# Gate biases of a hybrid block: one 128-row product of rounded parts and remainders in place of a narrow f32 product

## The chip, the cores and the metric

One Trainium2 chip, one core of it. The metric is the device time of one execution in microseconds (us), as the median of several executions. The kernel is one program that runs two transformer blocks, one after the other, on 256 tokens of width 1024.

## The reference

The first block is a three-branch mixer (a short convolution, a sparse attention called NSA, a gated delta net called GDN) and a mixture of experts; the second is a block with latent attention, a dense feed-forward, a state space mixer and a second mixture of experts. What the change touches is the merge of the three branches:

```python
branches = einsum('bsrc,rcd->bsrd', stack([y_a, y_n, y_g], axis=2), w_branch)
gates = sigmoid(h @ w_gate + b_gate).reshape(b, s, 3, dm)      # b_gate: 3072 values
merged = sum(gates * branches, axis=2)
return merged @ w_out
```

Here h is the normed input (256 x 1024), w_gate is 1024 x 3072, and b_gate is added to every token's row before the sigmoid.

## The kernel before, in words

Weights are f32 and come through a ring of four 2 MB slots, loaded by the SP queue (L139) in an order written out by hand. A slot is reloaded once its last reader has signalled. Large products are made in three products of rounded operands (type fp32r): ScalarE rounds a part of the weights to w_hi (L192), VectorE makes the remainder w_lo (L202), and TensorE multiplies hi by hi, lo by hi and hi by lo (L263 to L265).

A gate unit is 512 columns of w_gate for branch r (0 to 2) and half (0 or 1): six gate units, each with four weight parts. `merge_part` (L1132 on) numbers the steps: steps 0 to 3 of a half are the gate parts and steps 4 and 5 the branch parts. `merge_step_pe` does one step: for both token tiles of 128 rows, two chunks of 128 input features, three products each, twelve matmuls of 512 columns in all. In the fourth gate step (n == 3) it also adds the bias: for each token tile one product whose left side is one column of the identity over 6 rows, repeated 128 times, and whose right side is `rows512`, the bias as 6 rows of 512 values. Both are plain f32 (L1156). So there are 12 such products, and the profile shows each as two matmuls. The left side picks row 2r + half and copies it to all 128 tokens.

These steps are not made in one place. They are put between the small products of the serial stages, so that TensorE has work while other engines answer:

- GDN (about 117 to 258 us): branch 0. A triangular matrix is inverted in levels lv = 1 to 6. In each level TensorE makes a product Z, a merge step, two more products (XZ, ZX), and a second merge step, while VectorE subtracts them (`gdn_newton`, L1519 and L1521) and makes the next level's mask (L1486). TensorE waits for L1521 before the next level. The bias falls in the second step of levels 2 and 5.
- NSA (about 258 to 446 us): branch 2, half 0 before the attention, then branch 2, half 1 and the gates of branch 1 beside the 12 attention jobs, one step per job. In a job TensorE makes scores, the merge step, the transposes of the job two before, and the output of the job three before; VectorE scores and finishes (L1789, L1795 to L1804), ScalarE takes exponentials (L1570) and copies (L1583), and both also round weights.
- ScalarE takes the sigmoid of a finished gate (L1188), VectorE multiplies it with the branch into `merged` (L1207 to L1212), whose first write is at about 200 us.

The bias rows come with the 18 small loads that SP issues in `start_sync` behind the first four weight loads; all of them raise the signal `small`, which TensorE and ScalarE await at the start of GDN (L1283, L1387). VectorE's list for GDN (`gdn_dve`, L1436) begins with a wait for ScalarE's `ea`.

After NSA come the last branch products, the output projection, and the first mixture of experts (to about 1000 us). SP issues the first expert loads after every engine has finished NSA.

Of the kernel before, what the change touches and what calls it, by code (L numbers as in the profile page):

```python
# [342 lines left out]
def block(nc, A, out):  # L343
# [5 lines left out]
    def sb(name, shape, dt=F32, where=None):  # L349
        return (where or ctx).enter_context(nc.sbuf_tensor(name, shape, dt))  # L350
# [79 lines left out]
    thin = sb("thin", [P, NT, 32], where=mix)  # L430
    gates = sb("gates", [P, NT, 24], where=mix)
    h_mix = [sb(f"h_mix_{n}", [P, KD, T], F32R, where=mix) for n in ("hi", "lo")]
    rows512 = sb("rows512", [6, 512], where=mix)
    gd = ExitStack()
    qkvT = sb("qkvT", [P, 12, T], where=gd)
    zT = sb("zT", [P, 4, T], where=gd)
# [511 lines left out]
    def start_sync(s):  # L948
# [1 line left out]
            s.dma_start(dst, src).then_inc(*small.up(by=16))  # L950

        s.dma_start(pos_i[:, :], A["positions_2"][0].rearrange("(t p) -> t p", p=P)).then_inc(*positions.up(by=16))
        load(rows512[:, :], A["b_gate"].rearrange("l (r n) -> (l r) n", n=512))
        load(w_thin[:, :, 0:24], rows(w_in[:, O_NG:O_NG + 24]))
        load(w_thin[:, :, 24:32], rows(w_in[:, O_GB:O_GB + 8]))
        load(w_thin[:, :, 32:64], rows(ssm_in[:, 5120:5152]))
# [180 lines left out]
    def merge_step_pe(p, r, step):  # L1137
        half, n, u, part = merge_part(r, step)
        if n == 0 or n == 4:
            if n == 0:  # L1140
                sums_let_go(r, half)
            banks.take(p, "unit", u)
            banks.hold("unit", u)
        ps = banks.held_by("unit", u)
        hi, lo = split.take(p, part)
        h, k0, kt = (h_mix, 2 * n, KD) if n < 4 else (ys_, 2 * n - 8, 4)
        if n == 4:
            p.wait_ge(*branch_made(r))
        for t in range(NT):
            o = ps[:, t * 512:(t + 1) * 512]  # L1150
            for k in range(2):
                ins = split_product(p, o, tiles(h, k0 + k, slice(t * P, (t + 1) * P)), (hi[:, k, :], lo[:, k, :]),
                                    k0 + k == 0, k0 + k == kt - 1 and n > 3)
            if n == 3:
                row = 2 * r + half
                ins = p.matmul(o, ident[0:6, row:row + 1].to_broadcast([6, P]), rows512[:, :], start=False, stop=True)  # L1156
        ins.then_inc(*split.used.up())
        if r != 1 and n == 5:
            banks.let_go("unit", unit["gate", r, half])
        if r == 1 and step in (7, 4):  # L1160
            banks.let_go("unit", unit["gate", 1, 0 if step == 7 else 1])
# [274 lines left out]
    def gdn_dve(v):  # L1436
        st = S["gdn"]
        d = st.dve
        v.wait_ge(*st.act.of("ea"))
        for t in range(NT):  # L1440
            settle(v, v.tensor_tensor(g_[:, t, :], thin[:, t, 28:32], gdn_ab[:, 4:8], ADD), d)
# [2195 lines left out]
```

## Time and profile before

| | |
|---|---|
| median of 3 runs | 2491.43 us (2487.21 to 2493.35) |
| profiled execution, its own time | 2489.03 us |
| its span, first to last instruction | 2487.2 us |
| TensorE matmul busy | 2173.5 us, 12847 instructions |
| VectorE busy | 1424.4 us |
| ScalarE busy | 1157.9 us |
| mean granted TensorE clock | 0.948 |

The span is what the trace covers; the own time is the same execution by the device's timer. Engines are PE (TensorE matmul), PEld (TensorE weight load), DVE (VectorE), ACT (ScalarE), POOL (GpSimd), SPq (the queue of SyncE, which issues DMAs). Matmuls overlap in the array, so the time one takes of the engine is the distance from its start to the next one's start, not the duration in its row. A granted clock of 1.00 is 2.4 GHz, and 0.50 is 1.2 GHz; the clock takes one of the two at any moment, and a value between is the mean of a stretch.

### The profile page before, as it was taken

Reading aid. Unit: us, or ns where it says so; the run is one execution under the profiler, and the core shown is the slowest. Engines: PE = TensorE matmul, PEld = TensorE weight load, DVE = VectorE, ACT = ScalarE, POOL = GpSimd, SP = SyncE. Lnnn points to the kernel's source line nnn. Section 1 sums busy time; section 2 is a strip of 40 time slices with the busy share of each in tenths; the row PEclk is TensorE's granted clock in tenths of the full one; section 3 lists DMA queues with packets and bytes.
Section 4 is the critical chain, followed back from the end, with each engine's and each line's share of the span. In section 5 each row is a group of like instructions: output and inputs, shape, how many; then the busy total and the mean of one; then the engine's idle time right before and its main releaser. Section 6 shows DMA issues by size and latency. Waiting matters only on the chain.

```text
span 2487.2 us, 30921 instructions
## 1 busy us (share of the span) xinstructions
PE 2173.5 (87%) x12847; PEld 1670.1 (67%) x12847; DVE 1424.4 (57%) x1977; ACT 1157.9 (47%) x1520; POOL 43.5 (2%) x107
## 2 busy tenths in 40 slices
PE   7989899886665665889999998989999999999997
PEld 7977767741111112667998887778787787787875
DVE  3844635421111101435455756669888888888897
ACT  4432254210000001443443566547777777787775
POOL 0000200000000000000000000000000000000000
PEclk9999988988888888999999998999999999999999
DMA  8442741679999999376454321339989989989994
GB/s 270 169 172 100 247 176 68 238 314 409 409 409 409 409 409 349 140 289 219 170 187 169 136 102 68 119 127 338 355 329 330 372 315 348 354 317 366 335 335 186
DMA packets 267695, 656.78 MB, mean 264 GB/s; under 512 B 13454, under 2 KB 38546, under 8 KB 267544
## 3 DMA queue, kind: packets, MB, share of 16 engines
q1 hardware_dynamic: 266592, 652.90, 70.8%
q8 instruction: 106, 1.74, 0.3%
q10 hardware_dynamic: 952, 1.77, 0.2%
q14 instruction: 45, 0.37, 0.0%
HBM read 653.60 MB, written 1.05 MB: 263 GB/s over the span
## 4 chain that ended last, share of the span: by engine, by line
PE 68%; DMA 16%; DVE 9%; ACT 5%; issue 2%; POOL 0%; ACTq 0%; DVEq 0%; POOLq 0%; SPq 0%
PE psum L263 17%; PE psum L264 17%; PE psum L265 17%; PE psum L252 8%; DMA ring<-in_w_expert_down 5%; DMA ring<-in_w_expert_up 5%; DMA ring<-in_w_expert_gate 5%; PE psum L2385 2%; DVE w_lo L202 2%; PE psum L1099 1%; PE psum L259 1%; ACT w_hi L192 1%; PE psum L2407 1%; DMA ring<-in_ada_w 1%; PE psum L893 1%
## 5 line engine op out<-in xcount | busy, mean ns | idle before, releaser
L202 DVE TENSOR_TENSOR w_lo<-ring,w_hi 128x1024 fp32r<-128x1024 f32 (+1 forms) x778 | 905.5, 1179 | 383.3 <-ACT w_hi L192 367.8
L192 ACT CAST w_hi<-ring 128x1024 fp32r<-128x1024 f32 (+1 forms) x778 | 785.1, 1015 | 435.5 <-PE psum L265 431.1
L263 PE MATMUL psum<-w_hi,xg_hi 128*128 128x512 f32 (+1 forms) x768 | 294.6, 384 | 1.3 <-ACT xg_lo L2068 1.3
L265 PE MATMUL psum<-w_lo,xg_hi 128*128 128x512 f32 (+1 forms) x768 | 289.4, 377 | 0.0
L264 PE MATMUL psum<-w_hi,xg_lo 128*128 128x512 f32 (+1 forms) x768 | 289.4, 377 | 0.0
L2385 PE MATMUL psum<-ring,hT 128*32 128x512 f32 x960 | 145.9, 738 | 116.7 <-DMA ring<-in_w_expert_gate 64.0
L2385 PEld LDWEIGHTS psum<-ring,hT 128*32 128x32 f32 x960 | 29.6, 122 | 228.4 <-DMA ring<-in_w_expert_up 77.3
L263 PEld LDWEIGHTS psum<-w_hi,xg_hi 128*128 128x128 f32 x768 | 144.7, 188 | 31.1 <-issue 1.7
L264 PEld LDWEIGHTS psum<-w_hi,xg_lo 128*128 128x128 f32 x768 | 144.8, 189 | 29.4 <-issue 1.7
L265 PEld LDWEIGHTS psum<-w_lo,xg_hi 128*128 128x128 f32 x768 | 144.6, 188 | 29.2
L263 PE MATMUL psum<-w_hi,midT_hi 128*128 128x512 f32 x352 | 140.8, 400 | 4.0 <-DVE w_lo L202 4.0
L2237 DVE TENSOR_TENSOR x<-x,psum 128x1024 f32<-128x1024 f32 x14 | 17.1, 1221 | 217.6 <-PE psum L252 217.6
L264 PE MATMUL psum<-w_hi,midT_lo 128*128 128x512 f32 x352 | 139.5, 396 | 0.0
L265 PE MATMUL psum<-w_lo,midT_hi 128*128 128x512 f32 x352 | 139.5, 396 | 0.0
L2407 PE MATMUL psum<-ring,midT 128*32 128x512 f32 x480 | 70.9, 722 | 43.9 <-DMA ring<-in_w_expert_down 43.4
L259 PE MATMUL psum<-ident 128*128 128x128 f32 x624 | 87.6, 304 | 16.3 <-issue 8.7
L263 PE MATMUL psum<-h_f_hi,w_hi 128*128 128x256 f32 x352 | 99.9, 284 | 1.6 <-DVE h_f_lo L811 1.6
L264 PE MATMUL psum<-h_f_hi,w_lo 128*128 128x256 f32 x352 | 99.7, 283 | 0.0
L265 PE MATMUL psum<-h_f_lo,w_hi 128*128 128x256 f32 x352 | 99.6, 283 | 0.0
L259 PEld LDWEIGHTS psum<-ident 128*128 128x128 f32 x624 | 84.2, 218 | 19.3 <-issue 10.6
L263 PEld LDWEIGHTS psum<-w_hi,midT_hi 128*128 128x128 f32 x352 | 66.3, 188 | 20.8 <-issue 5.4
L2420 ACT COPY midT<-psum 128x512 f32<-128x512 f32 x8 | 4.7, 586 | 160.3 <-PE psum L893 160.3
(665 smaller groups left out, 3773.8 us busy)
## 6 DMA issues: line engine op xcount, KB each, us to landing
ring<-in_moe_w_gate SPq DMA_DIRECT2D x40, 2048.0 KB, 9.2
ring<-in_moe_w_up SPq DMA_DIRECT2D x40, 2048.0 KB, 10.0
ring<-in_moe_w_down SPq DMA_DIRECT2D x40, 2048.0 KB, 9.1
ring<-in_w_expert_gate SPq DMA_DIRECT2D x30, 2048.0 KB, 17.3
ring<-in_w_expert_up SPq DMA_DIRECT2D x30, 2048.0 KB, 17.1
ring<-in_w_expert_down SPq DMA_DIRECT2D x30, 2048.0 KB, 18.2
ring<-in_ada_w SPq DMA_DIRECT2D x24, 2048.0 KB, 8.6
ring<-in_ssm_w_in SPq DMA_DIRECT2D x10, 2048.0 KB, 8.0
```

What stands on the lines that cost most here:

```text
L192: a.copy(self.buffers(n, src.shape)[0], src).then_inc(*self.hi_made.up())
L202: v.tensor_tensor(lo, src, hi.bitcast(F32), SUB).then_inc(*self.lo_made.up())
L252: ins = p.matmul(o, l, r, start=n == 0, stop=n == len(terms) - 1)
L259: p.matmul(o[:, 0:P], constant[:, :], constant[:, :], start=True, stop=True)
L263: p.matmul(o, l[0], r[0], start=start, stop=False)
L264: p.matmul(o, l[1], r[0], start=False, stop=False)
L265: return p.matmul(o, l[0], r[1], start=False, stop=stop)
L893: ins = p.transpose(ps[0:c, n * P:n * P + r], src, ident[0:r, 0:r])
L1099: ins = p.matmul(ps[32 * quarter:32 * quarter + 32, 0:256], cond[:, k:k + 1].to_broadcast([P, 32]), w[quarter // 2][:, k, c0:c0 + 256], st ...
L2237: v.tensor_tensor(M.acc[:, t, :], M.acc[:, t, :], run.banks.of(st.name, "scatter", i, t), ADD).then_inc(*st.dve.up("acc", i, t))
L2385: ins = p.matmul(ps[slots_of(j), g * 512:(g + 1) * 512], M.xg[:, 2 * q + k, slots_of(j)], w[:, j, k, :], start=2 * q + k == 0, stop=2 * q ...
L2407: ins = p.matmul(ps[slots_of(j), cut], M.midT[:, q, slots_of(j)], w[:, j, cut], start=q == 0, stop=q == 3)
```

## The change

The bias is split into a rounded part and a remainder, both fp32r, that lie in one buffer of 128 rows: the rounded part in rows 0 to 5, the remainder in rows 32 to 37, zero elsewhere. A matrix `pick` (128 x 6) has ones at (p, p) and (32 + p, p). One product over 128 rows of a repeated column of `pick` with the buffer then adds both parts. SP loads the bias twice, into rows 0 to 5 and 32 to 37 of `merged`, which is not in use yet. VectorE makes `pick` and the buffer at the start of GDN in six operations, and TensorE waits for the last of them before each bias product.

```diff
-    rows512 = sb("rows512", [6, 512], where=mix)
+    rows512 = sb("rows512", [P, 512], F32R, where=mix)
+    pick = sb("pick", [P, 6], F32R, where=mix)
...
-        load(rows512[:, :], A["b_gate"].rearrange("l (r n) -> (l r) n", n=512))
+        for r in (0, 32):
+            load(merged[r:r + 6, 0, 0:512], A["b_gate"].rearrange("l (r n) -> (l r) n", n=512))
...
-                ins = p.matmul(o, ident[0:6, row:row + 1].to_broadcast([6, P]), rows512[:, :], start=False, stop=True)
+                p.wait_ge(*S["gdn"].dve.of("bias"))
+                ins = p.matmul(o, pick[:, row:row + 1].to_broadcast([P, P]), rows512[:, :], start=False, stop=True)
...
     def gdn_dve(v):
         st = S["gdn"]
         d = st.dve
+        v.wait_ge(*small.end())
+        v.tensor_tensor(pick[:, :], ident[:, 0:6], ident[:, 32:38], ADD).then_inc(*d.up())
+        settle(v, v.tensor_scalar(rows512[:, :], ident[:, 0:1].to_broadcast([P, 512]), 0.0, None, MUL), d)
+        v.tensor_copy(rows512[0:6, :], merged[0:6, 0, 0:512]).then_inc(*d.up())
+        settle(v, v.tensor_copy(rows512[32:38, :], merged[32:38, 0, 0:512]), d)
+        settle(v, v.tensor_tensor(rows512[32:38, :], merged[32:38, 0, 0:512], rows512[32:38, :].bitcast(F32), SUB), d, "bias")
         v.wait_ge(*st.act.of("ea"))
```

`settle` lets an operation signal and makes VectorE wait for that signal before its next one.

## Rows read from the trace of the kernel before

**Rows 1.** The page's chain that ended last, by engine.
```profile
PE 68%; DMA 16%; DVE 9%; ACT 5%; issue 2%; POOL 0%; ACTq 0%; DVEq 0%; POOLq 0%; SPq 0%
```
**Rows 2.** Busy time by stretch: us, each engine's busy (instructions), PEclk, DMA share, GB/s.
```profile
165.00:241.00 76.00, 72.92 (x440) 61.57 (x441) 34.11 (x30) 20.70 (x21) 0.00 (x0) 0.97 0.24 84
356.00:446.00 90.00, 82.61 (x415) 65.09 (x414) 48.10 (x138) 41.81 (x95) 0.00 (x0) 0.86 0.20 73
...
490.00:1000.00 510.00, 321.81 (x2084) 121.81 (x2084) 86.32 (x250) 37.70 (x61) 4.33 (x26) 0.88 0.97 384
...
430.00:446.00 16.00, 13.55 (x90) 10.57 (x88) 5.19 (x17) 4.64 (x6) 0.00 (x0) 0.98 0.00 1
```
**Rows 3.** The bias line's instructions: duration ns least/median/most, first and last start.
```profile
L1156 PEld LDWEIGHTS psum<-rows,ident x24: 180/183/328, 189.0 to 434.3; 6*128 6x128 f32 x24
L1156 PE MATMUL psum<-rows,ident x24: 587/691/1218, 189.0 to 434.7; 6*128 6x512 f32 x24
```
**Rows 4.** The chain by line, from 100 to 300 us, then from 300 to 480 us.
```profile
by line: PE psum L252 22.9%; PE psum L263 10.8%; PE psum L264 10.4%; PE psum L265 10.3%; PE psum L1099 6.8%; PE psum L259 3.6%; issue 3.5%; DVE w_lo L202 2.4%; PE psum L893 2.4%; PE psum L1156 2.1%; DVE dec L1486 1.8%; DVE shared L1521 1.7%
...
by line: PE psum L252 15.5%; PE psum L263 14.4%; PE psum L264 12.2%; PE psum L265 12.2%; PE psum L1156 5.2%; issue 4.0%; ACT w_hi L192 3.2%; PE psum L1548 3.1%; PE psum L1677 3.0%; ACT nsa_s L1570 2.5%; DVE nsa_s L1789 2.5%; DVE nsa_mx L159
```
**Rows 5.** Timeline of TensorE, a gate step without bias: start us, duration us, instruction.
```profile
175.41 0.48 PE L263 MATMUL psum<-w_hi,h_mix_hi 128*128 128x512 f32 x1
175.74 0.40 PE L264 MATMUL psum<-w_hi,h_mix_lo 128*128 128x512 f32 x1
...
178.30 0.50 PE L252 MATMUL psum<-ident,ada_row 128*128 128x4 f32 x4
179.29 0.35 PE L252 MATMUL psum<-shared,dec 128*128 128x128 f32 x1 [0.48 <-DVE shared L1521]
```
**Rows 6.** Timeline of TensorE, the step with bias of branch 0, half 0.
```profile
187.44 0.48 PE L263 MATMUL psum<-w_hi,h_mix_hi 128*128 128x512 f32 x1
...
189.01 1.12 PE L1156 MATMUL psum<-rows,ident 6*128 6x512 f32 x2
190.06 0.50 PE L263 MATMUL psum<-w_hi,h_mix_hi 128*128 128x512 f32 x1
...
192.71 2.05 PE L252 MATMUL psum<-shared,dec 128*128 128x128 f32 x16
```
**Rows 7.** Timeline: VectorE's last operation in levels 1, 2 and 5; TensorE after level 5.
```profile
177.97 1.22 DVE L1521 TENSOR_TENSOR shared<-shared,psum 128x1024 f32<-128x1024 f32 x1
...
189.99 1.21 DVE L1521 TENSOR_TENSOR shared<-shared,psum 128x1024 f32<-128x1024 f32 x1
...
227.77 1.22 DVE L1521 TENSOR_TENSOR shared<-shared,psum 128x1024 f32<-128x1024 f32 x1
...
230.49 2.05 PE L252 MATMUL psum<-shared,dec 128*128 128x128 f32 x16
```
**Rows 8.** Timeline: begin and hand-over of the step with bias of branch 2, half 0.
```profile
318.74 0.50 PE L263 MATMUL psum<-w_hi,h_mix_hi 128*128 128x512 f32 x1
...
327.13 3.66 PE L1099 MATMUL psum<-ring,cond 128*32 128x256 f32 x64
```
**Rows 9.** Timeline behind the step with bias of branch 2, half 1.
```profile
356.67 0.18 DVE L1795 RECIPROCAL wgt<-nsa_den 128x4 f32<-128x4 f32 x1 [2.29 <-PE psum L252]
...
358.41 0.79 PE L263 MATMUL psum<-w_hi,ys_hi 128*128 128x512 f32 x1
```
**Rows 10.** Timeline of VectorE behind the step with bias of branch 1, half 0.
```profile
404.48 0.18 DVE L1795 RECIPROCAL wgt<-nsa_den 128x4 f32<-128x4 f32 x1 [0.33 <-PE psum L252]
...
406.40 1.42 DVE L1789 SCALAR_TENSOR_TENSOR nsa_s<-dist,psum 128x256 f32<-128x256 f32 x4 [0.65 <-PE psum L252]
```
**Rows 11.** Timeline of ScalarE behind the step with bias of branch 1, half 1.
```profile
435.36 1.03 ACT L1188 ACTIVATE nsq<-psum 128x1024 f32<-128x1024 f32 x1 [3.84 <-PE psum L1156]
```
**Rows 12.** Timeline of VectorE, its first operation in GDN.
```profile
132.57 0.36 DVE L1441 TENSOR_TENSOR g<-thin,gdn_ab 128x4 f32<-128x4 f32 x2 [15.22 <-ACT ea L1395]
```
**Rows 13.** Timeline of SP's queue, the load of the bias.
```profile
19.36 0.27 SPq L950 DMA_DIRECT2D rows<-in_b_gate  x1
```

## The prediction

> **What bounds the kernel now.** I read the chain of waits first. Over the whole span it lies on TensorE for 68% and on DMA for 16% [rows 1]. Then I cut the span into stretches: between 165 and 446 us, where all twelve gate biases are added, TensorE is busy 96% and 92% of the time and DMA 24% and 20%; from 490 to 1000 us it is the reverse, DMA 97% [rows 2]. So the stretch that matters here is bound by TensorE and by the engines that hand work to it, and the DMA-bound expert stage comes after it. Just before that stage, from 430 to 446 us, DMA moves nothing [rows 2]: its first expert load waits for the end of the attention stage, so its start moves with whatever is gained earlier.
>
> Next, the product to be changed. The twelve bias products appear as 24 matmuls over 6 rows, 691 ns in the median [rows 3]: each f32 product runs as two passes. The chain says how much of them sets the end: L1156 is 2.1% of the 200 us from 100 to 300 and 5.2% of the 180 us from 300 to 480 [rows 4], that is 4.2 + 9.4 = 13.6 us, about twelve products at 1.05 and one of them at twice that. All lie on the chain. But a share of the chain is not a gain, so I look at each of the six steps (two products each).
>
> **The price of one product.** A gate step without bias, twelve matmuls of 512 columns, begins at 175.41 and hands over at 178.30: 2.89 us. Its matmuls follow each other at (178.30 - 175.74) / 11 = 0.233 us [rows 5]. The same step with bias runs from 187.44 to 192.71: 5.27 us. One pair of passes takes 190.06 - 189.01 = 1.05 [rows 6], and the change from one kind of product to the other and back adds the rest: (5.27 - 2.89) / 2 = 1.19 per product. The new product has the form of the others, 128 rows by 128 columns by 512, rounded operands, hence 0.233. A step becomes 2.89 + 2 x 0.233 = 3.36, saving 1.91 where TensorE alone decides.
>
> The Trainium skill ("FP8 and Floating Point Precision", TensorE Precision Notes) says a true f32 product is four passes. By that alone a product would cost 4 x 0.233 = 0.93 and the step would save 1.40; the trace shows 1.19, and it decides.
>
> **Step by step.** First a gate of branch 0, half 0 (187.44): the engine must next wait for VectorE's inverse step, which starts its last part at 189.99 and takes 1.21, so 191.20; in the earlier level the same operation ends at 177.97 + 1.22 = 179.19 and TensorE goes on at 179.29 [rows 5, 7], 0.10 later. So the next product starts at 191.30 in place of 192.71: 1.41 saved, and 0.5 us becomes a wait for VectorE. Half 1 is the same picture: VectorE is done at 227.77 + 1.22 + 0.10 = 229.09 against 230.49 [rows 7]: 1.40.
>
> Branch 2, half 0 begins at 318.74 and hands over at 327.13 [rows 8]: 8.39 us, much of it at the 1.2 GHz level. TensorE decides there and after it. I take 1.91, the full-clock price. At least 1.0, if the 64 matmuls behind it move into the half-clock stretch; at most 2.7, if both products are saved as they stand there.
>
> Branch 2, half 1 (just before 355 us): VectorE had been idle for 2.29 us when the work behind this step released it [rows 9], more than the 1.91, so all of it passes.
>
> Branch 1, half 0: here VectorE is nearly late. Before its two next operations it waits for TensorE only 0.33 and 0.65 us [rows 10]; its other inputs come through ScalarE's weight rounding, which does not move. 0.98 saved, the rest turns into a wait of TensorE.
>
> Branch 1, half 1: ScalarE sat idle 3.84 us for exactly this product [rows 11]. 1.91.
>
> **What is added.** VectorE gets six operations ahead of the delta-net's first one, at most 512 elements a lane. The largest row at hand, 1024 elements in 1.22 [rows 7], bounds them at 6 x 1.22 = 7.3 us; VectorE idles 15.22 us there for ScalarE [rows 12]. Cost nothing; without that cover, up to 7.3. Behind the new wait for the small loads stand only these six and that same idle. The small loads are long down: TensorE and ScalarE wait for the same signal already. SP issues one load more, 0.27 us [rows 13] and about 0.04 to the next; the small loads behind it and the first weight load after them slip by 0.3. The costliest lines of the chain from 100 to 300 us name no weight load [rows 4]. Cost nothing; 0.3 if bound. The two copies of the bias land in a buffer that is first written at about 200 us. TensorE gets twelve waits on a signal given 60 us before the first of them; queued behind each is the product and the rest of the step. The hand-over of the step without bias holds such waits too, inside its 2.89, so I take 0; at most 0.1 each (175.74 - 175.41 is 0.33 where 0.233 is usual, the largest small delay there [rows 5]), 1.2 in all. Loading the picked column repeated 128 times is not in the trace for rounded operands; the narrow one takes 183 ns [rows 3]. Hidden under the product before it, as the 0.233 spacing shows for the other loads, it costs 0; wholly exposed 12 x 0.18 = 2.2. Neither can be a gain, since the step holds twelve hidden loads already.
>
> **Sum.** 1.41 + 1.40 + 1.91 + 1.91 + 0.98 + 1.91 = 9.5 us. The profiled execution has a span of 2487.2 and a time of 2489.0; it would become 2477.7 and 2479.5. The median of the three runs is 2491.4, 2.4 above the profiled one, so the median becomes **2481.9**, 0.38% less. The three runs spread over 6.1 us; about 0.3%, 7.5 us, is what a measurement of this kernel can tell from no change.
>
> **Rivals.** *The clock gives part back.* Between 356 and 446 us the mean granted clock is 0.86 [rows 2]: 0.14 x 90 x 2 = 25 us at the 1.2 GHz level. A half-clock stretch costs step 8.39 - 5.27 = 3.1 us where it lies over one [rows 6, 8]. The change makes three waits longer (0.5, 0.5, 0.9 us). One stretch more, or one moved onto full work: gain 3 to 7.5, time 2484 to 2488.5. For it: one of the six steps already runs mostly at half clock [rows 8]. Against: the new waits stay below 1 us, and the clock is 0.97 in the stretch of two of them [rows 2]. 0.20. The Trainium skill ("TensorE: Matmul & The Clock Gate", HAM oscillation) says that idle gaps of TensorE bring the clock down to half; by it alone longer waits speak for this rival and shorter narrow products do not speak against it.
>
> *The clock adds.* The narrow products, 6 rows of 128, may count as little work of the array. If 128-row products spare one or two of them, 3 to 6 us more: 2476 to 2479. For it: right after the third of these steps a full-width matmul of 512 columns shows 0.79 us [rows 9] where one shows 0.48 at full clock [rows 5], so a drop follows a stretch that held two narrow products. Against: most of the narrow work around it stays. 0.12.
>
> *The product is not cheaper.* If the 128-row form with a repeated column ran in two passes as now, or the waits cost as much, the time stays at 2491, within 3. Nothing in the trace suggests it. 0.05.
>
> *Slower.* One mechanism: TensorE, with waits where it had f32 passes, drops to 1.2 GHz in the delta-net stretch, whose clock is 0.97 now [rows 2]. At 3.1 us for each step under it, three such stretches cancel the 9.5, and only with six (18.6) does the time reach 2500. With 76 us in the stretch and new waits of 0.5 that is far off. 0.03.
>
> My case, a gain between 7.5 and 13 us: 0.60. Faster by over 0.3%: 0.60 + 0.12 = 0.72; within 0.3%: 0.20 + 0.05 = 0.25; slower 0.03. The range takes in the clock cases and the low bounds (9.5 - 0.9 - 1.2 - 2.2 = 5.2, and some clock): 2476.5 to 2487.5.
>
> **What the changed profile would show.** Twelve matmuls of 128 by 512 at the bias line, 0.4 us each, starting 0.233 apart from their neighbours. The two delta-net bias steps ending in a wait for VectorE of about 0.5 us. Six short VectorE operations before 133 us, with 8 us or more idle left. At 400 us a wait of TensorE where there was none. The first expert load issued 9.5 us sooner, DMA busy from about 436, and every later stage as long as before. I would be wrong if the product took more than 0.5 us, if the shift at the first expert load were 9.5 but gone at 1000 us, or if the low-clock share between 165 and 446 us moved by more than 7 us.

## The result and the profile after

The kernel after takes 2475.89 us (median of 4 runs, 2475.74 to 2477.2), the kernel before 2490.56 in the same comparison: a ratio of 0.9937, 95% interval 0.9925 to 0.9949. It is faster, as forecast, but by 14.7 us in place of 9.5, and its median lies 0.6 us below the low end of the range. The direction held; a size didn't. Where the other 5 us come from is what the runs below look for.

The profiled execution took 2477.2 us with a span of 2475.4. I read its trace in the order of the prediction. First the new product. The bias line by its instructions (duration ns least/median/most, first and last start), to be held against [rows 3]:

```profile
L1159 PEld LDWEIGHTS psum<-rows,pick x12: 187/188/329, 189.3 to 424.3; 128*128 128x128 f32 x12
L1159 PE MATMUL psum<-rows,pick x12: 392/397/628, 189.6 to 424.5; 128*128 128x512 f32 x12
```

Twelve matmuls where there were 24. The timeline of TensorE over the step of branch 0, half 0, the counterpart of [rows 6]:

```profile
188.08 0.47 PE L263 MATMUL psum<-w_hi,h_mix_hi 128*128 128x512 f32 x1
...
189.34 0.40 PE L265 MATMUL psum<-w_lo,h_mix_hi 128*128 128x512 f32 x1
189.57 0.40 PE L1159 MATMUL psum<-rows,pick 128*128 128x512 f32 x1
189.81 0.40 PE L263 MATMUL psum<-w_hi,h_mix_hi 128*128 128x512 f32 x1
...
191.21 0.40 PE L1159 MATMUL psum<-rows,pick 128*128 128x512 f32 x1
191.95 2.02 PE L252 MATMUL psum<-shared,dec 128*128 128x128 f32 x16 [0.35 <-DVE shared L1530]
```

The bias product starts 0.23 behind its neighbour and the next one 0.24 behind it. Then TensorE waits for VectorE's inverse step, as forecast: 191.95 - 188.08 = 3.87 us in place of 5.27, 1.40 saved. The next view is the same engine at branch 2, half 0, the counterpart of [rows 8]:

```profile
316.85 0.51 PE L263 MATMUL psum<-w_hi,h_mix_hi 128*128 128x512 f32 x1
...
318.90 0.63 PE L1159 MATMUL psum<-rows,pick 128*128 128x512 f32 x1
...
321.53 0.40 PE L1159 MATMUL psum<-rows,pick 128*128 128x512 f32 x1
321.86 3.66 PE L1101 MATMUL psum<-ring,cond 128*32 128x256 f32 x64
```

5.01 us in place of 8.39: 3.38 saved where I had taken 1.91 and bounded it by 2.7. In the trace of before the same step holds 6.8 us of half clock; the timeline shows it by the spacing:

```profile
320.66 0.63 PE L265 MATMUL psum<-w_lo,h_mix_hi 128*128 128x512 f32 x1
321.22 2.07 PE L1156 MATMUL psum<-rows,ident 6*128 6x512 f32 x2
323.22 0.80 PE L263 MATMUL psum<-w_hi,h_mix_hi 128*128 128x512 f32 x1
```

One old product at 1.2 GHz took 323.22 - 321.22 = 2.0 us. In after the low clock ends at about 321.0 inside the step, and its first bias product takes 0.43.

SP's queue shows when the expert stage may begin. From the timeline of the kernel after, SP:

```profile
19.13 0.61 SPq L951 DMA_DIRECT2D merged<-in_b_gate  x2
...
435.33 0.92 SPq L128 DMA_DIRECT2D place_ns<-in_w_expert_gate  x2
```

and of the kernel before:

```profile
445.89 0.92 SPq L128 DMA_DIRECT2D place_ns<-in_w_expert_gate  x2
```

10.6 us earlier, 1.1 more than the sum. Over 165 to 446 us the mean granted clock is 0.93 in before and 0.95 in after, about 39 and 28 us at 1.2 GHz; that moved by more than the 7 us that the prediction had set as a sign of being wrong, though the trace of e_same has 0.93 again. At the end of the expert stage it is more again. TensorE from the last expert product to the transposes of the next norm, before:

```profile
975.94 3.70 PE L252 MATMUL psum<-ysb,selgT 128*128 128x512 f32 x8 [1.14 <-ACT ysb L2428]
983.19 0.49 PE L259 MATMUL psum<-ident 128*128 128x128 f32 x2 [3.54 <-issue]
988.86 4.64 PE L259 MATMUL psum<-ident 128*128 128x128 f32 x20 [5.19 <-issue]
993.29 2.78 PE L822 MATMUL psum<-ident,xn_mla 128*128 128x128 f32 x16
```

and after:

```profile
963.61 3.70 PE L252 MATMUL psum<-ysb,selgT 128*128 128x512 f32 x8 [1.13 <-ACT ysb L2437]
970.70 3.36 PE L259 MATMUL psum<-ident 128*128 128x128 f32 x14 [3.39 <-issue]
976.37 2.08 PE L259 MATMUL psum<-ident 128*128 128x128 f32 x8 [2.31 <-issue]
978.24 2.72 PE L823 MATMUL psum<-ident,xn_mla 128*128 128x128 f32 x16
```

L259 here is eleven constant products that only keep TensorE busy. In both kernels TensorE stops in the middle of them and waits for nothing that the trace shows ("issue"): in before behind 2 of the 22 matmuls, in after behind 14. The piece lasts 17.35 us in before and 14.63 in after, so 2.7 us are won some 540 us behind the last bias product. At 1014 us (by the clock of before) the two kernels stand 15.1 us apart; the 121 us behind that differ by 3.3 the other way, at a mean granted clock of 0.95 in after and 0.97 in before. From 1135 us on both traces take the same 1352.1 us.

The additions cost nothing that the trace shows. There are five VectorE operations, not the six that the description of the change and the prediction count (L1443 to L1447 in the timeline of after, the counterpart of [rows 12]):

```profile
117.07 0.16 DVE L1443 TENSOR_TENSOR pick<-ident 128x6 fp32r<-128x6 f32 x1
...
118.49 0.68 DVE L1447 TENSOR_TENSOR rows<-merged,rows 6x512 fp32r<-6x512 f32 x1
132.13 0.36 DVE L1450 TENSOR_TENSOR g<-thin,gdn_ab 128x4 f32<-128x4 f32 x2 [12.96 <-ACT ea L1398]
```

### The profile page after: what moved, and what is told of

The parts are those of the page before. It is cut to its first block, busy times and chain, and to the rows that moved or that the text cites. A ratio compares the mean times of both kernels' runs of the same rounds, so it can differ in the third digit from the quotient of the medians.

```text
span 2475.4 us, 30904 instructions
## 1 busy us (share of the span) xinstructions
PE 2179.2 (88%) x12835; PEld 1674.8 (68%) x12835; DVE 1426.1 (58%) x1982; ACT 1157.8 (47%) x1520; POOL 43.5 (2%) x107
## 3 DMA queue, kind: packets, MB, share of 16 engines
HBM read 653.61 MB, written 1.05 MB: 264 GB/s over the span
## 4 chain that ended last, share of the span: by engine, by line
PE 67%; DMA 16%; DVE 10%; ACT 5%; issue 2%; POOL 0%; ACTq 0%; DVEq 0%; POOLq 0%; SPq 0%
PE psum L263 17%; PE psum L264 16%; PE psum L265 16%; PE psum L252 8%; DMA ring<-in_w_expert_up 5%; DMA ring<-in_w_expert_down 5%; DMA ring<-in_w_expert_gate 5%; PE psum L2394 2%; DVE w_lo L202 2%; PE psum L1101 2%; ACT w_hi L192 1%; PE psum L259 1%; PE psum L2416 1%; DMA ring<-in_ada_w 1%; PE psum L894 1%
## 5 line engine op out<-in xcount | busy, mean ns | idle before, releaser
L192 ACT CAST w_hi<-ring 128x1024 fp32r<-128x1024 f32 (+1 forms) x778 | 785.2, 1015 | 435.9 <-PE psum L265 431.6
L2394 PE MATMUL psum<-ring,hT 128*32 128x512 f32 x960 | 161.5, 807 | 101.8 <-DMA ring<-in_w_expert_gate 58.1
L259 PE MATMUL psum<-ident 128*128 128x128 f32 x624 | 87.6, 304 | 13.3 <-ACT z L3182 7.6
L259 PEld LDWEIGHTS psum<-ident 128*128 128x128 f32 x624 | 84.1, 218 | 16.4 <-ACT z L3182 8.3
## 6 DMA issues: line engine op xcount, KB each, us to landing
ring<-in_w_expert_gate SPq DMA_DIRECT2D x30, 2048.0 KB, 17.4
ring<-in_w_expert_up SPq DMA_DIRECT2D x30, 2048.0 KB, 17.2
```

The source lines that it names most:

```text
L192: a.copy(self.buffers(n, src.shape)[0], src).then_inc(*self.hi_made.up())
L259: p.matmul(o[:, 0:P], constant[:, :], constant[:, :], start=True, stop=True)
L2394: ins = p.matmul(ps[slots_of(j), g * 512:(g + 1) * 512], M.xg[:, 2 * q + k, slots_of(j)], w[:, j, k, :], start=2 * q + k == 0, stop=2 * q ...
```

## The experiments

Step C below is the step of branch 2, half 0; **the C piece** runs from its first matmul to the first of the next bias step, branch 2, half 1 (in before 318.74 to 349.70, in after 316.85 to 344.42). **The end piece** runs from the last expert product (L252, `ysb`) to the transposes at L822/L823. Names of kernels are those of the runs.

### The additions, and the kernel after again

e_setup is the kernel after with the old product; the bias's remainder is left out of its result.

```diff
-                ins = p.matmul(o, pick[:, row:row + 1].to_broadcast([P, P]), rows512[:, :], start=False, stop=True)
+                ins = p.matmul(o, ident[0:6, row:row + 1].to_broadcast([6, P]), rows512[0:6, :].bitcast(F32), start=False, stop=True)
```

> All that the change adds (two loads, six VectorE operations, the twelve waits of TensorE), but the product stays the f32 one over 6 rows, with the rounded part of the bias alone as its right side, so the remainder is left out of the sum. Both theories: the additions are hidden, time as the kernel before within 1.5 us, 2489 to 2492. If the additions cost what I bounded: up to 2 us slower. If it is faster than before, something among the additions (the early shift of loads, the VectorE work) gives part of the 14.7.

Measured: 2490.47 (12 runs) against 2491.43 (17 runs), ratio 0.9999 (0.999 to 1.0007). The loads, the five VectorE operations and the twelve waits cost nothing beyond the interval, which reaches 2.5 us to either side; the gain of 14 to 15 us comes with the product.

e_same is the kernel after, unchanged.

> The changed kernel as it is, once more. Theory W (only TensorE's time in the six steps counts, 9.5 us; the rest of the 14.7 is where the half-clock stretches happened to fall in the few executions compared): with more executions the difference of the medians falls towards 10 us, ratio 0.996, and the runs of the kernel before spread over 5 us or more. Theory R (the products over 6 rows pull the clock down, the 128-row ones don't): the difference stays at 13 to 15 us, ratio 0.994 to 0.995.

Measured: 2477.57 (2474.56 to 2480.23), ratio 0.9947 (0.9934 to 0.996), 13.9 us gained. It puts the gain of after at 14 to 15 us, against theory W, and shows that five runs of one kernel spread over 5.7. That the gain lasts does not by itself show theory R, that the rows pull the clock down.

### Passes or rows

Two things differ between the products: f32 or rounded operands, 6 rows or 128. e_wide_f32 has 128 rows and plain f32, e_narrow_r 6 rows and rounded operands (the remainder is left out of its result).

```diff
-    rows512 = sb("rows512", [P, 512], F32R, where=mix)
-    pick = sb("pick", [P, 6], F32R, where=mix)
+    rows512 = sb("rows512", [P, 512], F32, where=mix)
+    pick = sb("pick", [P, 6], F32, where=mix)
```

> The changed kernel with both buffers in f32: 128 rows, two passes. The time of the passes should stay 1.05 us and a product 1.19. Theory W: same as before, 2489 to 2491, ratio 0.999 to 1.001. Theory R: the rows are full, so the clock holds better at the same work: 3 to 5 us faster than before, 2485 to 2487, and fewer half-clock microseconds between 165 and 446 us than the 54.6 - 17.1 = 37 of the kernel before.

```diff
-                ins = p.matmul(o, pick[:, row:row + 1].to_broadcast([P, P]), rows512[:, :], start=False, stop=True)
+                ins = p.matmul(o, pick[0:6, row:row + 1].to_broadcast([6, P]), rows512[0:6, :], start=False, stop=True)
```

> The changed kernel with its product cut to rows 0 to 5: rounded type, one pass, 6 rows, so the remainder is left out of the sum. Theory W: exactly the time of the changed kernel, 2475 to 2478. Theory R: one pass of 0.233 us over 6 rows is idle for the clock: 1 to 4 us slower than the changed kernel, 2478 to 2480.

Measured: 2479.08 (ratio 0.9955, 0.9942 to 0.9968) and 2477.41 (0.9943, 0.993 to 0.9956). For e_wide_f32 both theories missed: it gains 12.4 us where W had 0 to 2 and R 3 to 5. Its profiled execution is its slowest of five (2483.97) and has the first expert load at 443.00. e_narrow_r came out as W had it, level with after. The medians are too close to tell the two apart, the steps are not. TensorE in e_narrow_r, branch 0, half 0:

```profile
189.59 0.40 PE L265 MATMUL psum<-w_lo,h_mix_hi 128*128 128x512 f32 x1
189.92 0.49 PE L1159 MATMUL psum<-rows,pick 6*128 6x512 f32 x1
190.34 0.50 PE L263 MATMUL psum<-w_hi,h_mix_hi 128*128 128x512 f32 x1
190.68 0.39 PE L264 MATMUL psum<-w_hi,h_mix_lo 128*128 128x512 f32 x1
```

and in e_wide_f32:

```profile
190.87 0.39 PE L265 MATMUL psum<-w_lo,h_mix_hi 128*128 128x512 f32 x1
191.09 1.02 PE L1159 MATMUL psum<-rows,pick 128*128 128x512 f32 x2
191.55 0.80 PE L263 MATMUL psum<-w_hi,h_mix_hi 128*128 128x512 f32 x1
192.19 0.40 PE L264 MATMUL psum<-w_hi,h_mix_lo 128*128 128x512 f32 x1
```

A narrow product makes its own start and those of the next two matmuls late, each 0.33, 0.42 and 0.34 behind the one before where 0.233 is usual; the wide f32 product doesn't delay its own start. From whole steps (time above the 2.89 of a step without bias, over two) a product costs 1.19 us narrow f32, 0.87 wide f32, 0.57 narrow rounded, 0.233 wide rounded. So the row count is worth about 0.33 and the second pass 0.62 to 0.64, and they add. The prediction had the right sum and put 1.05 of it down to the two passes and 0.14 to the change between kinds of product; the change of rows is more than twice that. The Trainium skill ("FP8 and Floating Point Precision", TensorE Precision Notes), by which f32 is four passes, fits the wide product: 0.87 is 3.7 times 0.233. The narrow one is above it by what the change of rows costs.

### Which step the gain comes from

The new product in step C alone, everywhere but in C, in branch 0 alone, and everywhere but in branch 0. Each is the kernel after with a condition of this form, the old product in the else branch:

```diff
+                if (r, half) == (2, 0):
                     ins = p.matmul(o, pick[:, row:row + 1].to_broadcast([P, P]), rows512[:, :], start=False, stop=True)
+                else:
+                    ins = p.matmul(o, ident[0:6, row:row + 1].to_broadcast([6, P]), rows512[0:6, :].bitcast(F32), start=False, stop=True)
```

> Only the step of branch 2, half 0 gets the new product (its two of twelve); the other ten stay narrow f32, with the rounded part of the bias alone, so the remainder is left out there. Theory W: 1.9 us faster than before at full clock, 2489 to 2490. Theory K (the wide product lets the half-clock stretch over this step end 3.4 us or more earlier; so far 6.8 to 13.7 us of half clock in the three traces with the narrow product, 3.4 in the three with the wide one): 3.5 to 6 us faster, 2485.5 to 2488, and 3.4 us of half clock in the trace between 315 and 350 us.

> The reverse: ten new products, and the two of branch 2, half 0 stay narrow f32, with the rounded part alone. Theory W: 1.9 us slower than the changed kernel, 2478 to 2480. Theory K: 3.5 to 6 us slower, 2480 to 2483, with 6.8 us or more of half clock over that step.

> The new product in the two delta-net steps (branch 0) alone, the old one in the other four. By the steps' own prices 2.8 us under the kernel before, near 2488.5. Rival, what is gained there is multiplied behind it by the clock: 5 us or more, 2486 or less. Rival, the clock phase eats it: 0 to 1.5 us.

> The new product in the four steps of branches 2 and 1, the old one in the two delta-net steps. By the measured prices of the steps (3.4 with step C and the piece behind it, 1.9, 0.2, 1.9) 7.4 us under the kernel before, near 2484; if gains do not add and the clock settles the rest, 10 to 14 us, 2477 to 2481. Together with the run of branch 0 alone: their sum is 14.7 if gains add, less or more if the clock's part belongs to neither alone.

| run | median us | kernel before | ratio (interval) | first expert load at | C piece |
|---|---|---|---|---|---|
| e_c_only | 2482.31 | 2491.7 | 0.9958 (0.9944 to 0.9971) | 443.40 | 27.6 |
| e_not_c | 2477.15 | 2491.7 | 0.9941 (0.9928 to 0.9955) | 437.50 | 31.0 |
| e_branch0 | 2483.02 | 2492.2 | 0.9963 (0.9949 to 0.9976) | 447.57 | 34.3 |
| e_rest | 2475.05 | 2492.2 | 0.9935 (0.9921 to 0.9949) | 438.81 | 27.6 |

Every median is lower than its steps explain, and the halves don't add to the whole by medians: 9.4 + 14.6 and 9.2 + 17.2 against 14.7. Both theories missed for e_not_c: with the old product left in C it is level with after (2477.15 against 2475.89 and 2477.57), so by medians the new product in C is worth nothing there, and 9.4 us in e_c_only. So the time behind the steps is not fixed. Up to the first expert load they do better. Four traces with the old product everywhere issue it at 445.89, 447.79, 448.59 and 449.12, mean 447.8; three with the new one at 435.33, 435.93 and 436.33, mean 435.9: 12.0 apart. Step C alone wins 4.4 and the rest 10.3; branch 0 alone 0.3 and the rest 9.0. Single traces differ by 3 us here, so these numbers carry no more than that. Of the 12.0, 0.9 already lies ahead of the first bias step, where nothing was changed. The other 11.1 by stretches, means of the same four and three traces: from the first bias step to C 3.1 us, the C piece 5.1, from branch 2, half 1 to branch 1, half 0 1.5, from there to half 1 0.5 the wrong way, and from there to the first expert load 2.0.

What stands out is the C piece. With the old product in C, unfilled, it took 31.0 us (before, e_not_c), 32.6 (e_before_again, e_before_shift; the expectation of e_before_again knew only 31.0 and 34.3) or 34.3 (e_setup, e_branch0, e_before_fill): seven traces, mean 32.9. With the new product it took 27.6 in all seven traces that have it rounded and nothing filled ahead of C (after, e_same, e_c_only, e_rest, the two fillings of the attention, e_after_shift). The granted clock differs with it. Windows over exactly the C piece (us, busy time of PE, PEld, DVE, ACT and POOL, PEclk, DMA share, GB/s), of before:

```profile
318.78:349.74 30.96, 30.96 (x178) 21.33 (x177) 11.72 (x26) 15.67 (x39) 0.00 (x0) 0.89 0.28 100
```

of e_setup:

```profile
318.98:353.28 34.30, 34.30 (x178) 22.01 (x178) 11.49 (x26) 15.66 (x39) 0.00 (x0) 0.80 0.26 90
```

and of after:

```profile
316.92:344.49 27.57, 27.57 (x176) 20.93 (x175) 11.74 (x26) 15.68 (x39) 0.00 (x0) 0.94 0.31 112
```

TensorE is busy throughout in each. The time at 1.2 GHz is (1 - 0.89) x 30.96 x 2 = 6.8 us, 0.20 x 34.30 x 2 = 13.7 and 0.06 x 27.57 x 2 = 3.3. The old product doesn't only cost more at half clock, the low clock also lasts longer with it.

### No bias product

e_none leaves the bias of the gates out.

```diff
-            if n == 3:
-                row = 2 * r + half
-                p.wait_ge(*S["gdn"].dve.of("bias"))
-                ins = p.matmul(o, pick[:, row:row + 1].to_broadcast([P, P]), rows512[:, :], start=False, stop=True)
```

> The changed kernel without any bias product: b_gate is left out of the result; VectorE's preparation stays. It bounds what the product can still cost. Both theories: the two steps in the delta net wait for VectorE anyway, so only three or four steps gain 0.47 each: 1.4 to 1.9 us faster than the changed kernel, 2474 to 2476. If the product's clock effect matters beyond its time, it can come out slower than that, since full work goes away.

Measured: 2470.6 (2469.75 to 2476.36), ratio 0.9917 (0.9904 to 0.9931). It is 5 us below after, where the twelve products hold 2.8 and 1.4 to 1.9 were expected. Its C piece is 27.1 us. In its end piece the 22 constant matmuls run in one go and the piece lasts 11.2 us, 3.4 less than in after. That is of the size of the rest, and it pointed at the end piece.

### Holding the clock in the attention stage

Constant products in two waits of the attention, on the kernel after (twice) and on the kernel before:

```diff
                 if len(jobs) <= n < len(jobs) + AHEAD:
                     constant_products(p, ps[:, 512:1024], ident, 5)
+                if st.name == "nsa" and n in (4, 10):
+                    constant_products(p, ps[:, 512:1024], ident, 24)
```

> The changed kernel plus 24 small products of constants (about 2.8 us, results unused) behind the outputs of attention jobs 4 and 10, where the changed kernel's TensorE idles 3.2 and 3.4 us for ScalarE and then runs at half clock. Theory K, applied there: the clock stays up, 2 to 4 us faster than the changed kernel, 2473 to 2475.5. Theory W: no change, 2475 to 2478, or 1 us slower if the filling outlasts the wait.

> The kernel after with 24 constant products in each of the attention steps 4 and 10, once more, beside its counterpart on the kernel before, so that both share the runs of the kernel before. By the first run of this edit: 22 to 25 us under the kernel before, 2465 to 2470.

> The kernel before with the 24 constant products in each of the attention steps 4 and 10, as in the filled version of the kernel after. Theory 1, the surplus over 9.5 us comes from how the half-clock stretches fall in the attention stage: with the attention filled, before and after lie closer together than 14.7 us; if all of the surplus sits there, before filled is about 9.5 us above after filled (2468), near 2478. Rival, the surplus is the narrow products' own, wherever the clock stands (step C and the expert stage included): before filled is 13 to 15 us above after filled, near 2482, and the filling is worth no more here than in the kernel after (8 to 9 us).

Measured: e_fill 2468.09 (ratio 0.99, 0.9885 to 0.9915), e_fill_again 2470.27 (0.9913, 0.9897 to 0.9928), e_before_fill 2485.07 (0.997, 0.9958 to 0.9982). The distance between filled kernels is 14.8, as between unfilled ones. So the surplus is not in the attention stage, and my first theory of it fell. The filling itself gave 6 to 9 us on after where I had expected 2 to 4; about 3 of them are there at the first expert load (432.47 and 433.18 against 435.9), and its end pieces last 11.2 and 12.7 us. The 96 added matmuls also move the stall that is looked at below, so this gain is not the clock's alone. In e_before_fill the first expert load isn't earlier at all (448.36); its 7 us come at the end piece, which lasts 11.7 us in place of 17.4.

### Holding the clock ahead of step C

TensorE waits 7.11 us for VectorE ahead of the compression product, 17 us before C. Timeline of before:

```profile
301.98 1.29 PE L1677 MATMUL psum<-ring,fl 128*32 128x128 f32 x20 [7.11 <-DVE fl L1832]
```

The edit, on before (e_before_hold) and on after (e_after_hold); e_best has it together with the filled attention steps, on after:

```diff
+        ps = banks.take(p, "cmp")
+        constant_products(p, ps, ident, 28)
         p.wait_ge(*st.dve.of("fl"))
...
-        ps = banks.take(p, "cmp")
```

> The kernel before with 28 constant products in the 7.1 us in which TensorE waits for VectorE ahead of the compression product (L1677). Theory, the surplus is the half clock over step C: C then runs at full clock and costs its 5.27 in place of 8.39, C with the piece behind it at most 28 us in place of 31 to 34.3; the kernel gains 3 to 6 us, near 2487. Rival, the clock at C is set by what stands directly ahead of it and not by that wait: the half-clock stretch is still over C and the time is that of before within 2 us, or higher by what the products delay.

> The kernel after with the same 28 constant products. Theory: C costs 3.36 in place of 5.0; the kernel gains 1 to 3 us over after (2476), and lies 10 to 12 us below e_before_hold, since at full clock the new product is worth 1.91 at C. Rival: it lies 14 to 15 us below e_before_hold as after does below before.

> The kernel after with both fillings, ahead of the compression product and in attention steps 4 and 10. If they add: 1 to 3 us below the attention filling alone (2468 to 2470), 2466 to 2468. If the clock's phase decides anew: anything between 2464 and 2474.

> The kernel before unchanged, for a second trace. Median 2491 to 2492. Step C with the piece behind it, up to branch 2's second bias step, costs 31.0 or 34.3 us in traces with the old product; which of the two shows here is open, and that it is one of them and not 27.6 is what the theory of the surplus needs.

| run | median us | ratio (interval) | first expert load at | C piece |
|---|---|---|---|---|
| e_before_hold | 2476.19 | 0.9941 (0.9928 to 0.9955) | 438.89 | 27.9 |
| e_after_hold | 2469.89 | 0.9914 (0.99 to 0.9927) | 433.18 | 27.6 |
| e_best | 2467.53 | 0.9897 (0.9882 to 0.9913) | 430.40 | 26.0 |
| e_before_again | 2492.42 | 1.0001 (0.9992 to 1.001) | 447.79 | 32.6 |

Timeline of e_before_hold at the same place:

```profile
293.78 6.41 PE L259 MATMUL psum<-ident 128*128 128x128 f32 x56
301.14 3.70 PE L1678 MATMUL psum<-ring,fl 128*32 128x128 f32 x128 [0.95 <-DVE fl L1833]
```

and its window over the C piece:

```profile
316.07:343.94 27.87, 27.87 (x178) 19.84 (x177) 11.56 (x26) 15.68 (x39) 0.00 (x0) 1.00 0.32 110
```

The clock stays at 2.4 GHz through C with the old product in place, and the piece takes 27.9 us in place of 31.0 to 34.3. The kernel before, with 28 products that compute nothing, is as fast as the kernel after, 15.6 us below before where I had expected 3 to 6: 9 us are won at the first expert load (447.8 to 438.9; 1.5 of them already lie ahead of the first bias step; the rest is the compression product itself at full clock, 3.70 in place of 5.42, and the C piece), the rest at the end piece, which lasts 9.8 us since no stall falls among the 22 constant matmuls. On after the same edit wins 6.0 us by medians where 1 to 3 were expected: 2.7 (435.9 to 433.2) and then 3.0 at the end piece. Between the two held kernels 6.3 us are left of 14.7, less than the 10 to 12 that I had written down: e_after_hold still had 3.4 us of half clock over C (window 0.94), where e_best had none, and its piece was 27.6 in place of 26.0. At full clock on both sides the piece differs by 27.9 - 26.0 = 1.8 us, which is the 1.91 of the prediction. The Trainium skill ("TensorE: Matmul & The Clock Gate", HAM oscillation) names idle gaps of TensorE as what brings the clock down; over the compression product, right behind the gap of 7.1 us, the trace agrees: 3.70 us in all three held traces, 5.1 to 6.2 in the others.

Over C the cause is not settled by these runs. In before the low clock is not one stretch from the gap to C. Windows of before:

```profile
303.00:306.00 3.00, 3.00 (x72) 2.80 (x68) 2.45 (x10) 0.00 (x0) 1.21 (x2) 0.57 0.00 0
309.00:312.00 3.00, 3.00 (x24) 2.68 (x23) 0.29 (x1) 0.92 (x3) 0.00 (x0) 1.00 0.93 345
321.00:324.00 3.00, 3.00 (x5) 1.18 (x5) 0.43 (x1) 0.00 (x0) 0.00 (x0) 0.50 0.61 225
```

The clock is back at 2.4 GHz from about 306 to 319 us and falls again inside C, behind a second wait of 1.57 us directly ahead of it (L1699, for VectorE's `kc`), which every one of these traces has. And e_after_hold and e_best have the same instructions up to the end of the C piece (the attention fillings come behind it), yet one has the low clock over C and the other doesn't. The C piece of e_after_hold:

```profile
314.78:342.37 27.59, 27.59 (x176) 20.83 (x175) 12.02 (x30) 15.38 (x37) 0.00 (x0) 0.94 0.31 111
```

So with the gap filled the clock held over C in two of three traces, and without it in none of the seventeen others; what decides between them is open.

### Moving the stall at the end of the expert stage

In the traces so far the stall fell behind 2 of the 22 constant matmuls with 24 bias matmuls in the program (before, e_setup, e_wide_f32), behind 4, 6, 10 and 12 with 2, 4, 8 and 10 fewer (e_c_only, e_branch0, e_rest, e_not_c), behind 14 with 12 fewer (after, e_same, e_narrow_r), and there was none among the 22 with 24 fewer (e_none). In e_none it lies 0.64 us long behind 3 of the 16 transposes that follow, 25 matmuls in where the rule gives 26. Two runs move that point by 12 matmuls the other way, through constant products at 20 to 28 us that a wait for VectorE covers: 24 in place of 18 in after, 12 in place of 18 in before.

```diff
-            by_feature_pe(p, unit["conv", n], h_mix, ready=None if n else st.dve.of("h", 4), begin=None if n else st.dve.of("h", 0), idle=0 if n else 18)
+            by_feature_pe(p, unit["conv", n], h_mix, ready=None if n else st.dve.of("h", 4), begin=None if n else st.dve.of("h", 0), idle=0 if n else 24)
```

> The kernel after with 24 in place of 18 constant products (12 matmuls more) in the wait ahead of the first projection. Theory, the stall at the end of the expert stage sits at a fixed place in TensorE's instructions: it moves from behind 14 of the 22 constant matmuls back to behind 2, and the piece from the last expert product to the transposes lasts 17.4 us in place of 14.7; median 2.7 above after, near 2479. Rival, the stall is set by what the DMA queues do at that time: it stays behind 14, the piece stays at 14.7 and the time at 2476 to 2477.

> The kernel before with 12 in place of 18 constant products there (12 matmuls fewer). Theory: the stall moves from behind 2 to behind 14, the piece lasts 14.7 us in place of 17.4, median 2.7 below before, near 2489. Rival: both stay, 2491 to 2492.

The end piece of e_after_shift:

```profile
974.55 0.79 PE L259 MATMUL psum<-ident 128*128 128x128 f32 x2 [4.95 <-issue]
980.36 4.63 PE L259 MATMUL psum<-ident 128*128 128x128 f32 x20 [5.02 <-issue]
984.79 2.16 PE L823 MATMUL psum<-ident,xn_mla 128*128 128x128 f32 x16
```

and of e_before_shift:

```profile
979.04 3.70 PE L252 MATMUL psum<-ysb,selgT 128*128 128x512 f32 x8 [1.14 <-ACT ysb L2428]
986.23 1.83 PE L259 MATMUL psum<-ident 128*128 128x128 f32 x14 [3.49 <-issue]
991.87 2.08 PE L259 MATMUL psum<-ident 128*128 128x128 f32 x8 [3.82 <-issue]
993.74 2.38 PE L822 MATMUL psum<-ident,xn_mla 128*128 128x128 f32 x16
```

Both stalls moved as written down: behind 2 in after, with a piece of 18.9 us (17.4 expected), and behind 14 in before, with 14.7. So its place follows the number of matmuls ahead of it. The time follows less clearly. e_before_shift took 2491.17 against 2493.2 of the kernel before, 0.999 (0.9982 to 0.9999), 2.0 us less. e_after_shift took 2479.16, the figure expected, but the kernel before was slower in this comparison too: it is 14.0 us below it, ratio 0.9948 (0.9935 to 0.9961), and e_same without the edit had 13.9 and 0.9947. Its trace loses 4.2 us at the end piece and wins as much behind it (1491.5 us from the transposes to the end, against 1495.5 and 1497.2 in e_same and after). Side by side the two shifted kernels lie 12.0 apart, where 14.7 and 13.9 had been measured.

What TensorE waits for in the stall is argued, not shown. While it stands in before (983.7 to 988.9) the last of a full stretch of weight load drains and a packet moves on a queue of the kind "instruction", but such packets are also there in stretches without a stall (979 to 983 and 989 to 993 in before), so they don't single it out.

The stall ends 12.4 to 13.6 us behind the start of the last expert product wherever it began (988.86 - 975.94 = 12.9 in before, 976.37 - 963.61 = 12.8 in after, 12.4 in e_none; only in e_after_shift 14.5), so what lies ahead of it is free and what lies behind it is paid. The Trainium skill ("Runtime: NRT & Kernel Launch", Instruction fetch mechanics) says that an engine's instructions are refilled in blocks of fixed size by a DMA of their own, and that this is mostly hidden. A stall at a fixed place in the instructions agrees with the blocks; "hidden" doesn't hold here, at 2.3 to 5.3 us a time.

## Why the prediction was wrong where it was

**Branch 0, both halves (1.41 and 1.40).** Right: 5.27 to 3.87 in each, with the wait for VectorE that was named.

**Branch 2, half 0 (1.91, 1.0 to 2.7).** The step that failed. It was costed at full clock, though [rows 8] showed the step at half clock, and even its upper bound kept the low clock's length fixed. Measured 3.4 in the profiled pair; over seven traces on each side the piece takes 32.9 and 27.6, 5.3 less. Where the clock held on both sides (e_before_hold and e_best) the piece differs by 1.8, the full-clock price, so the other 3.5 go with the length of the low clock. That is shown in the traces of the piece; the median of e_not_c, level with after, does not show it in the time. The second term that the sum lacked is the end piece, below.

**Branch 2, half 1 (1.91).** Right: 5.29 to 3.38, and the piece behind it is not longer.

**Branch 1, half 0 (0.98).** Too high. The step itself fell from 5.31 to 3.37, but TensorE then waits; in the timeline of after:

```profile
391.11 1.97 PE L252 MATMUL psum<-kv,dup 128*128 128x64 f32 x16 [0.28 <-DVE yn L1813]
...
396.25 0.79 PE L263 MATMUL psum<-w_hi,h_mix_hi 128*128 128x512 f32 x1 [1.25 <-ACT kcT L1592]
```

The second wait is for ScalarE's copy (L1592), a hand-over that the prediction did not look at: it set aside ScalarE's weight rounding as not moving and looked at VectorE alone. Step and piece behind took 9.99 us before and 9.82 (after, e_after_shift) or 9.17 (e_same): 0.2 to 0.8 saved; over the longer stretch to the next bias step nothing was.

**Branch 1, half 1 (1.91).** Right: 5.27 to 3.36; ScalarE's wait shrank from 3.84 to 2.02.

**Additions (0).** Right: VectorE keeps 12.96 us idle, and e_setup is level with before. With five operations the bound would have been 6.1 us in place of 7.3; nothing hangs on it.

**The clock adds (0.12, 2476 to 2479).** This rival was the likeliest as it turned out, and its mechanism, a shorter low clock with fewer narrow products, agrees with the C piece. But it looked for it behind branch 2, half 1 (the fourth of the steps, not the third as it says), and that its figure of 2476 to 2479 lies next to the measured 2475.89 is in part luck: some 3 us come from the low clock over C and 2 to 3 from a stall that it did not know of. **The clock gives part back (0.20)** had the longer waits right and the sign wrong up to the expert stage; a loss of its kind shows only behind 1014 us, 3.3 us in the profiled pair, and the time from the transposes to the end varies from 1491.5 to 1497.2 us over all traces without following the product. **Slower** and **not cheaper** had nothing in them.

**What no case had.** The expert stage was taken as a fixed shift. It ends with a stall whose place depends on how many matmuls the program issues before it, and this change removed 12: 2.7 us in the profiled pair's traces, of which the shifted kernels show some 2 in the time. With 12.0 at the first expert load and 12.65 at the last expert product (means of the traces above, 977.7 and 965.0), that makes 15.3 where 14.7 were measured; the stretch behind it swings by 3 us in either direction, so that the sum comes out this close is partly chance.

**Open.** Why the low clock over C lasts 6.8 us in some traces and 13.7 in others with the old product and never more than 3.4 with the new one was not separated into rows, passes and duration: e_narrow_r gave 29.6 us and 6.8 of half clock, e_wide_f32 28.9 and 3.4, so the longer low clock goes with the 6 rows, but that is one trace each. Whether the 7.1 us wait or the 1.6 us one ahead of C brings it down there is open too. And why the four kernels with the product in part of the steps run 4 to 8 us below the sum of their pieces is not explained. The traces of two of them show some of it away from any bias step: in e_rest the expert stage, from its first load to the last expert product, lasts 526.2 us where the four traces with the old product everywhere have 528.1 to 530.7, and behind the transposes e_rest and e_not_c take 1492.4 and 1492.7 us where those four take 1493.9 to 1496.5.

## What to carry to other kernels

Cost an edit at the clock at which its place runs, and ask how long the low clock would last with the new work; constant products in a long wait are a cheap thing to try (28 of them in before brought the first expert load 7 to 9 us forward; both fillings on after gave 2467.53 us, no clear gain over the 2468.09 and 2470.27 of the attention filling alone). Behind a stage that keeps the DMA queues full, look for "issue" stalls of TensorE and note behind how many instructions they fall before a small edit is credited with its time. Judge parts by the steps and by a fixed event such as the first expert load, since here medians of five runs moved by 4 to 8 us with what their steps don't explain.

## What the hardware showed that was not expected

- A product over 6 rows between products over 128 costs 0.33 us more than one over 128, beside its passes.
- With TensorE busy throughout and no filling ahead of it, the C piece kept 6.8 to 13.7 us of half clock with two narrow f32 products in it and 3.4 with 128-row ones.
- The clock was back at 2.4 GHz for some 12 us between a low stretch behind a 7.1 us wait and the one over C, and one and the same list of instructions up to there had the second low stretch in one trace (e_after_hold) and not in another (e_best).
- TensorE's stall at the end of the expert stage follows the number of matmuls ahead of it exactly: behind 2, 4, 6, 10, 12 or 14 of the 22 constant matmuls with 0, 2, 4, 8, 10 or 12 fewer ahead, in thirteen traces without exception, and two edits moved it back and forth as written down.
